# Three phases over the sequence, with Strassen's seven products in gate/up and down

## What is computed

```python
hn = rmsnorm(x, norm_mix_g)
q, k, v, r, a_low = split(hn @ w_in)                 # 512, 512, 1024, 1024, 16 columns
log_a = log_sigmoid(a_low @ w_a2 + b_a) / 16         # decays, summed up within chunks
...                                                  # scores in a chunk, a state carried from chunk to chunk
o = rmsnorm(o, gla_norm_g) * silu(r)
h = x + o @ w_out
g, u = split(rmsnorm(h, norm_ffn_g) @ w_gu)          # 2816 columns each
h = h + (silu(g) * u) @ w_down
out = rmsnorm(h, final_norm_g)
```

## Time and profile before

| | |
|---|---|
| median of 3 runs | 2424.64 us (2423.86 to 2426.31) |
| span of the profiled execution | 2424.4 us |
| TensorE busy | 2348.6 us, 97% |
| GpSimd busy | 1553.0 us, 64% |
| VectorE busy | 718.2 us, 30% |
| ScalarE busy | 539.1 us, 22% |
| mean granted TensorE clock | 0.986 of full |
| DMA | 236 MB, mean 97 GB/s |

### The profile page before, as it was taken

One profiled execution on the slowest core, in us unless ns is written; L12 is line 12 of the kernel. 1 busy time (PEld: TensorE's weight loads), 2 busy tenths in 40 slices (PEclk: granted clock), 3 DMA queues, 4 the chain that ended last, 5 costly groups with the idle time before them and its releaser, 6 DMA issues.

```text
span 2424.4 us, 33041 instructions
## 1 busy us (share of the span) xinstructions
PE 2348.6 (97%) x10948; PEld 1956.8 (81%) x10948; DVE 718.2 (30%) x1119; ACT 539.1 (22%) x871; POOL 1553.0 (64%) x1592
## 2 busy tenths in 40 slices
PE   6999999999899999999989999999998999999997
PEld 5888888888788788888778878888877888888885
DVE  5342311013534321011364431101245343110125
ACT  3331220011333222001133312200132232220114
POOL 6555677676656566677675557667766656677673
PEclk8999999999999999999999999999999999999998
DMA  4322333333422233233342223323334223332332
GB/s 142 106 65 91 96 96 102 97 95 110 135 78 78 78 108 100 96 95 95 105 140 70 86 87 99 100 96 95 95 96 139 87 72 99 98 95 96 95 97 85
DMA packets 298924, 236.26 MB, mean 97 GB/s; under 512 B 15104, under 2 KB 260864, under 8 KB 298848
## 3 DMA queue, kind: packets, MB, share of 16 engines
q1 hardware_dynamic: 290224, 209.44, 28.0%
q10 hardware_dynamic: 8624, 25.76, 2.9%
HBM read 226.76 MB, written 8.39 MB: 97 GB/s over the span
## 4 chain that ended last, share of the span: by engine, by line
PE 90%; DVE 5%; issue 2%; ACT 1%; DMA 1%; POOL 0%; DVEq 0%; ACTq 0%; POOLq 0%
PE ps L386 28%; PE ps L388 28%; PE ps L387 28%; PE ps L434 1%; PE ps L499 1%; DVE lc L909 1%; DVE xs L846 1%; PE ps L470 1%; PE ps L474 1%; DMA xs<-in_x 1%; PE ps L507 1%; DVE lc L906 1%; PE ps L443 0%; DVE newton L828 0%; PE ps L444 0%
## 5 line engine op out<-in xcount | busy, mean ns | idle before, releaser
L378 POOL TENSOR_TENSOR ring_lo<-raw,ring_hi 128x512 fp32r<-128x512 f32 x784 | 1030.6, 1315 | 65.3
L375 POOL TENSOR_SCALAR ring_hi<-raw 128x512 fp32r<-128x512 f32 x784 | 515.2, 657 | 762.8 <-PE ps L388 528.2
L386 PE MATMUL ps<-xT_hi,ring_hi 128*128 128x512 f32 (+1 forms) x1728 | 664.6, 385 | 8.3 <-DVE xT_lo L815 8.3
L387 PE MATMUL ps<-xT_lo,ring_hi 128*128 128x512 f32 (+1 forms) x1728 | 661.7, 383 | 0.0
L388 PE MATMUL ps<-xT_hi,ring_lo 128*128 128x512 f32 (+1 forms) x1728 | 661.6, 383 | 0.0
L386 PEld LDWEIGHTS ps<-xT_hi,ring_hi 128*128 128x128 f32 x1728 | 327.3, 189 | 72.1 <-issue 9.9
L388 PEld LDWEIGHTS ps<-xT_hi,ring_lo 128*128 128x128 f32 x1728 | 327.4, 189 | 62.8
L386 PE MATMUL ps<-ring_hi,act_hi 128*128 128x512 f32 x960 | 377.2, 393 | 0.8 <-POOL ring_lo L378 0.7
L387 PEld LDWEIGHTS ps<-xT_lo,ring_hi 128*128 128x128 f32 x1728 | 327.3, 189 | 62.5
L388 PE MATMUL ps<-ring_hi,act_lo 128*128 128x512 f32 x960 | 374.6, 390 | 0.0
L387 PE MATMUL ps<-ring_lo,act_hi 128*128 128x512 f32 x960 | 374.3, 390 | 0.0
(11 more groups left out here) (114 smaller groups left out, 1767.0 us busy)
## 6 DMA issues: line engine op xcount, KB each, us to landing
raw<-in_ffn_w_gu SPq DMA_DIRECT2D x352, 256.0 KB, 3.1
raw<-in_gla_w_in SPq DMA_DIRECT2D x192, 256.0 KB, 3.0
raw<-in_ffn_w_down SPq DMA_DIRECT2D x176, 256.0 KB, 3.1
raw<-in_gla_w_out SPq DMA_DIRECT2D x64, 256.0 KB, 3.0
h<-in_x ACTq DMA_DIRECT2D x16, 512.0 KB, 6.4
xs<-in_x ACTq DMA_DIRECT2D x16, 512.0 KB, 3.5
out<-xs ACTq DMA_DIRECT2D x8, 512.0 KB, 4.3
h<-in_x SPq DMA_DIRECT2D x4, 512.0 KB, 6.9
```

The lines of the kernel that those rows point to most:

```text
L375: pool.tensor_scalar(ring_hi[:, u, :], raw[:, p, u % 2, :], 1.0, 0.0, ALU.mult, ALU.add).then_inc(unit_hi[u].sem, 1)
L378: pool.tensor_tensor(ring_lo[:, u, :], raw[:, p, u % 2, :], ring_hi[:, u, :].bitcast(F32), ALU.subtract).then_inc(unit_split[u].sem, 1)
L386: pe.matmul(out, l_hi, r_hi, start=first, stop=False)
L387: pe.matmul(out, l_hi, r_lo, start=False, stop=False)
```

## The change

The program is fully unrolled and runs in three phases over the whole sequence: the mixer for all four blocks; then gate/up for all tokens; then down for all tokens, with the final norm. What passes from one to the next goes through DRAM tensors: `xop` (operands of gate/up), `hop` (hidden operands of down), `hres` (the residual). The sequence counts as NS = 2 halves of 1024 tokens.

A product of 2x2 blocks is made with seven instead of eight block products (the form of Strassen and Winograd). The blocks halve the tokens, the inner dimension and the columns. The sums of activation blocks are made once and stored with high and low parts (7 operands); the sums of weight blocks are made by GpSimd anew for each use. A "quad" is the weights for 2x2 blocks (four quarters of 128 x 512 numbers, 1 MB); its seven products take 84 matmuls. There are 44 quads in gate/up and 22 in down. Even quads of gate/up are gate, odd ones up; two make a pair. The output sums lie in PSUM banks that are used twice, so some products wait until VectorE has read a bank (`bank_free`).

GpSimd, for each quad: four sums and seven low parts.

```diff
+            def split_op(q, i):
+                pool.wait_ge(op_hi[i], q + 1)
+                pool.tensor_tensor(shaped(q, w_op[i][:, 1, :]), source(q, i), shaped(q, w_op[i][:, 0, :]).bitcast(F32),
+                                   ALU.subtract).then_inc(op_ready[i], 1)
+            for q in range(QUADS):
+                b11, b12, b21, b22 = quarters(q)
+                t2, t3 = shaped(q, w_t2[:, :]), shaped(q, w_t3[:, :])
+                pool.wait_ge(w_loaded[q % 2], 64 * (q // 2 + 1))
+                pool.tensor_tensor(t3, b22, b12, ALU.subtract).then_inc(t3_done, 1)
+                pool.wait_ge(t3_done, q + 1)
+                pool.tensor_tensor(b12, b12, b11, ALU.subtract).then_inc(t1_done, 1)
+                pool.wait_ge(t1_done, q + 1)
+                pool.tensor_tensor(t2, b22, b12, ALU.subtract).then_inc(t2_done, 1)
+                for i in range(5):
+                    split_op(q, i)
+                pool.wait_ge(op_ready[4], q + 1)
+                pool.tensor_tensor(b21, b21, t2, ALU.subtract).then_inc(t4_done, 1)
+                for i in (5, 6):
+                    split_op(q, i)
```

TensorE, gate/up:

```diff
+            def bank_free(lane, i):
+                if i == 3:
+                    pe.wait_ge(u2_done, lane + 1)
+                elif i == 4:
+                    pe.wait_ge(p1_kept, lane + 1)
+                elif i == 5:
+                    pe.wait_ge(u3_done, lane + 1)
+                elif i == 6:
+                    pe.wait_ge(c22_done, lane + 1)
+                elif lane < 2:
...
+            for q in range(U_QUADS):
+                B = q // (2 * NP)
+                for i in range(7):
+                    pe.wait_ge(op_ready[i], q + 1)
+                    if q % (2 * NP) == 0:
+                        pe.wait_ge(op_loaded[i], 64 * (B + 1))
+                    bank_free(q, i)
+                    for m in range(4):
+                        cols = slice(m * P, (m + 1) * P)
+                        ins = three(ps[:, 3 * (q % 2) + BANK[i], :], w_op[i][:, 0, cols], w_op[i][:, 1, cols],
+                                    x_op[i][:, m, 0, :], x_op[i][:, m, 1, :], m == 0 and i < 3, m == 3, i > 2)
+                    ins.then_inc(prod[i], 1)
+                    if q == 0 and i < NT:
+                        turn_result(NB - 1, i)
```

ScalarE, gate/up: the high parts of the weights, the loads of the x operands and the order of its queue (`switch` is the last quad of the first half of the tokens):

```diff
+            def op_split(q, i):
+                if i == 0 or i == 4 or i == 6:
+                    act.wait_ge(w_loaded[q % 2], 64 * (q // 2 + 1))
+                else:
+                    act.wait_ge({1: t2_done, 2: t1_done, 3: t3_done, 5: t4_done}[i], q + 1)
+                if q > 0:
+                    act.wait_ge(prod[i], lanes_end[q - 1])
...
+                split_hi(shaped(q, w_op[i][:, 0, :]), source(q, i)).then_inc(op_hi[i], 1)
+            def load_op(B, i, m):
+                act.dma_start(x_op[i][:, m, :, :].bitcast(F32), xop[B, i, :, m, :, :]).then_inc(op_loaded[i], 16)
+            def copy_p1(q):
+                act.wait_ge(prod[0], q + 1)
+                if q > 0:
+                    act.wait_ge(c21_done, q)
+                act.activation(x1[:, :], ps[:, 3 * (q % 2), :], ACT.Copy).then_inc(p1_kept, 1)
...
+            for q in range(U_QUADS):
+                B, pair = divmod(q // 2, NP)
+                pair = q // 2
+                switch = q == 2 * NP - 1
+                def next_op(i):
+                    op_split(q + 1, i)
+                    if switch:
+                        if i == 0:
+                            for slot in range(2):
+                                act.wait_ge(xop_stored[slot], 16 * (PER_BLOCK // 2) * NB)
+                        for m in range(4):
+                            load_op(1, i, m)
+                copy_p1(q)
...
+                elif q % 2 == 0:
+                    next_op(0)
+                    hidden_hi(pair - 1, 5)
+                    next_op(1)
+                    next_op(2)
+                    hidden_hi(pair - 1, 6)
+                    next_op(3)
+                    gate_silu(pair, 0)
+                    next_op(4)
+                    gate_silu(pair, 1)
+                    next_op(5)
+                    gate_silu(pair, 2)
+                    next_op(6)
+                    gate_silu(pair, 3)
+                else:
+                    next_op(0)
+                    next_op(1)
+                    if q == 1:
+                        result_granules(NB - 1, range(5, 7))
+                    next_op(2)
+                    if q == 1:
+                        result_granules(NB - 1, range(7, 10))
+                    next_op(3)
+                    if q == 1:
+                        result_granules(NB - 1, range(10, 14))
+                        for slot in range(2):
+                            act.wait_ge(xop_stored[slot], 16 * (PER_BLOCK // 2) * NB)
+                    hidden_hi(pair, 0)
+                    next_op(4)
+                    hidden_hi(pair, 1)
+                    next_op(5)
+                    hidden_hi(pair, 2)
+                    next_op(6)
+                    hidden_hi(pair, 3)
+                    hidden_hi(pair, 4)
```

VectorE, gate/up, the odd quad and the beginning of the next pair (`lane_u2` of the even one releases product 3 there):

```diff
+            def lane_u2(lane):
+                dve.wait_ge(p1_kept, lane + 1)
+                dve.wait_ge(prod[1], lane + 1)
+                dve.tensor_tensor(u2[:, :], ps[:, 3 * (lane % 2) + 1, :], x1[:, :], ALU.add).then_inc(u2_done, 1)
+            def lane_u3(lane):
+                dve.wait_ge(prod[3], lane + 1)
+                dve.tensor_tensor(u3[:, :], ps[:, 3 * (lane % 2) + 1, :], x1[:, :], ALU.add).then_inc(u3_done, 1)
+            def lane_22(lane, dst):
+                dve.wait_ge(u3_done, lane + 1)
+                dve.wait_ge(prod[2], lane + 1)
+                dve.tensor_tensor(dst[:, :], ps[:, 3 * (lane % 2) + 2, :], u3[:, :], ALU.add).then_inc(c22_done, 1)
+            def lane_21(lane, dst):
+                dve.wait_ge(prod[5], lane + 1)
+                dve.tensor_tensor(dst[:, :], ps[:, 3 * (lane % 2) + 1, :], x1[:, :], ALU.add).then_inc(c21_done, 1)
...
+            def times_gate(pair, tile, silu, ready, made):
+                dve.wait_ge(silu_done, 4 * pair + silu)
+                dve.wait_ge(ready, 2 * pair + 2)
+                dve.tensor_tensor(tile[:, :], tile[:, :], ct[:, :], ALU.mult).then_inc(made, 1)
+            def hidden_lo(pair, n):
+                number = 7 * pair + n
+                dve.wait_ge(hid_hi, number + 1)
+                split_lo(stage[number % 4][:, 1, :], (g22, g11, s1, g21, s2, g12, s4)[n][:, :],
+                         stage[number % 4][:, 0, :]).then_inc(hid_lo, 1)
+            def hidden_end(pair):
+                hidden_lo(pair, 5)
+                dve.wait_ge(hid_made, 7 * pair + 6)
+                dve.tensor_tensor(s4[:, :], g12[:, :], s2[:, :], ALU.subtract).then_inc(hid_made, 1)
+                hidden_lo(pair, 6)
...
+            for pair in range(U_QUADS // 2):
+                lane = 2 * pair
+                lane_u2(lane)
+                if pair > 0:
+                    hidden_end(pair - 1)
+                lane_u3(lane)
+                lane_22(lane, g22)
...
+                lane = 2 * pair + 1
+                lane_u2(lane)
...
+                lane_22(lane, ct)
+                times_gate(pair, g22, 1, c22_done, hid_made)
+                dve.wait_ge(silu_done, 4 * pair + 2)
+                dve.wait_ge(prod[4], lane + 1)
+                dve.tensor_tensor(g11[:, :], g11[:, :], ps[:, 3, :], ALU.mult).then_inc(c11_done, 1)
+                dve.wait_ge(c11_done, pair + 1)
+                dve.sem_inc(hid_made, 1)
...
+                hidden_lo(pair, 0)
+                hidden_lo(pair, 1)
+                lane_21(lane, ct)
+                times_gate(pair, g21, 3, c21_done, d21_done)
+                dve.wait_ge(d21_done, pair + 1)
+                dve.tensor_tensor(s1[:, :], g21[:, :], g22[:, :], ALU.add).then_inc(hid_made, 1)
+                dve.wait_ge(hid_made, 7 * pair + 3)
+                dve.tensor_tensor(g21[:, :], g11[:, :], g21[:, :], ALU.subtract).then_inc(hid_made, 1)
+                hidden_lo(pair, 2)
+                dve.tensor_tensor(s2[:, :], s1[:, :], g11[:, :], ALU.subtract).then_inc(hid_made, 1)
+                hidden_lo(pair, 3)
+                hidden_lo(pair, 4)
+                lane_12(lane, ct)
+                times_gate(pair, g12, 4, c12_done, hid_made)
+            hidden_end(U_QUADS // 2 - 1)
```

The pieces of `xop`, made in the first three heads of the next block, or for the last block in quads 0 and 1 of gate/up:

```diff
+            def result_hi(b, n):
+                kg, i = X_GRANULES[n]
+                number = PER_BLOCK * b + n
+                if i in (1, 2, 3, 6):
+                    act.wait_ge(xs_sum, 4 * (2 * b + kg) + {2: 1, 3: 2, 1: 3, 6: 4}[i])
+                else:
+                    act.wait_ge(xf_done, 2 * NT * (b + 1))
+                if number >= 2:
+                    act.wait_ge(xop_stored[number % 2], 16 * (number // 2))
+                split_hi(x_stage[b // (NB - 1)][:, number % 2, :, 0, :], x_source(kg, i)).then_inc(xop_hi, 1)
+            def result_store(b, n):
+                kg, i = X_GRANULES[n]
+                number = PER_BLOCK * b + n
```

(66 more changed lines are left out.)

## The result

The changed kernel takes **2498.5 us** (median of 4 runs, 2494.5 to 2503.0) where the kernel before, run beside it, takes 2424.3 us: a ratio of 1.031, 95% interval 1.029 to 1.032. It is slower by 74 us. The profiled execution has a span of 2496.4 us.

A forecast was written before the change was run, and what follows sets the result against it. TensorE's matmuls, with TensorE busy 97% of the span, were taken as the bound. Savings led by -179.5 us of products and added costs led by +114 summed to +77 on 2424, giving 2501 us; own range 2445 to 2560, overall 2365 to 2560.

The forecast's parts named there:

- GpSimd and VectorE in gate/up: Gate/up: GpSimd and VectorE lock each other out, making u2 late; 6.0 us in each of 19 pairs, +114 us.
- Storing the operands: Heads of the next block: ScalarE's pieces each wait for a store's landing and delay v_hi; +62 us, ends 30 and 95.
- New block borders: Between mixer blocks: late decay chain and first scaled tile, +25 us; norm_next ahead of v_lo in the last head, +27 us.
- Entry into gate/up: Start of gate/up: late weights, open norm, and last block's pieces ahead of copy_p1 on ScalarE; +38 us, ends 15 and 55.
- Change of half: After quad 21 of gate/up: reloading seven operands, 14.7 MB, takes 55 us and stops TensorE; +24 us, ends 8 and 40.
- Down: Down phase: DMA traffic fits and VectorE's gathers avoid the port, leaving 2 us for entries; +2 us, ends 0 and 45.
- Ends: Behind the last matmul: additions, squares, roots, scalings and the last store take 27 us instead of 17.4; +10 us.
- Products: Gate/up and down: 5544 matmuls instead of 6336, each 0.2267 us; -179.5 us.
- Rival 1: Gate/up: the port costs nothing because VectorE's 8.1 us chain stays inside 10.9 us; 2387 us, chance 0.17.
- Rival 2: Whole kernel: everything is covered, stores and squares too hide behind the matmuls; 2235 us, chance 0.05.
- half effect: Stores and gate/up: landing 2.9 us, 2 us stop per pair, too short to lower the clock; 2393 to 2440 us, chance 0.16.
- Rival 4: Down: DMA becomes the bound at 220 GB/s, pairs of quads taking 42 instead of 38 us; 2546 us, chance 0.12.

The follow-up runs named there:

- e1_order: Changed kernel with only VectorE's order in gate/up altered, lane_u2 of the next even quad ahead of hidden_lo 3 and 4: 2389.6 us, ratio 0.985.
- e2_no_gpsimd: Changed kernel without GpSimd's sums and low parts in gate/up from the third quad on, semaphores still raised: 2387.2 us, ratio 0.986.
- e8_both: Changed kernel with the edits of e1_order and e2_no_gpsimd together: 2385.4 us.
- e3_granules: Changed kernel with two operand pieces per head left ahead of v_hi, the others moved behind r_gate and into the recurrence's gaps: 2439.7 us, ratio 1.006.
- e4_norm: Changed kernel with three of norm_next's four multiplications moved behind v_lo in the last head of the first three blocks: 2485.7 us, ratio 1.026.
- e7_no_end: all1 without the sums, splits and stores of the last block's 14 operand pieces in the first two quads of gate/up: 2288.4 us.
- all1: Changed kernel with the order changes of e1_order, e3_granules and e4_norm together, nothing left out: 2315.6 us, ratio to before 0.955.
- e5_no_reload: all1 without the 28 loads of the second half's operands between the halves of gate/up: 2299.4 us.

## Why the prediction was right, point by point

The forecast was 2501 us, the measured median 2498.5. The sum is closer than its terms; four of them were off by more than 10 us and cancelled.

- **GpSimd and VectorE in gate/up, +114.** Right in mechanism (e1_order, e2_no_gpsimd, e8_both) and nearly in size: 19 pairs x 5.34 = 101.5 us. Inside it two parts were off in opposite ways. TensorE had finished product 2 at 1320.0, 8.3 us into the even quad, and `u2` was made at 1322.96, 11.3 us into it and not 12.6; the stop was 3.2 us, not 4.4. The clock cost 2.1 us on average, not 1.6, and from 0.1 to 3.0 us in single pairs: in the longest case it stayed at the lower level for some 6 us, against some 3 behind the 2.0 us pause of the earlier trace rows, and in two of the 19 it did not fall, so that it did not dip "in every pair". What decides between them no run here shows. The reason that the Trainium skill gives ("SBUF — State Buffer", section "SBUF: two separate sides"), that such instructions of the two engines shut each other out for a whole instruction, agrees with these runs: the same instruction takes 1.77 us beside GpSimd and 0.69 without it, and those that read PSUM take 0.68 in the same microseconds.
- **Storing the operands, +62.** 57.5 us in the trace, 58.8 given back by e3_granules. The sum for one piece was too high: a landing plus a split were counted, 4.25 us, but the split runs while the store before it is landing, and the pieces start 3.3 to 3.5 us apart. So `v_hi` starts 16.4, 13.6 and 10.4 us behind the scores in the second block's heads, against 17.5, 16 and 11.5. In the last block it is 17.7, 15.3 and 13.0 us, so that the three blocks pay 15.4, 19.0 and 23.3 us, where 21 had been set for each; why the later ones pay more is open. The whole cost was order.
- **New block borders, +25 and +27.** Too high: about 13 us a border and not 17. TensorE's waits between two blocks are 6.6 us for `v_lo`, 2.6 for the turned result and 0.5, 9.7 us in all, and 3 for the clock (99.3 us busy at 0.97). `v_lo` was late as said (6.6 against 7); e4_norm gives the border back 4.1 to 5.6 us of it. The step that failed is the first scaled tile, which the decay chain was to leave open for 5 us: TensorE does not wait for it at all, only for 2.6 us between the tiles.
- **Entry into gate/up, +38.** Too low, about 49. By the mark `s<-g,g` at 1094.93 and its place 37.3 us behind the start of an undisturbed pair (e1_order), gate/up would have had to begin at 1057.6; the output projection ended at 1004.7. Of the 52.9 us between, 3.6 are transposes counted elsewhere. e7_no_end confirms 27 us for the pieces, as predicted (28). The other item, 10 us for weights and norm, was nearer 22.
- **Change of half, +24.** 25.1 us by the marks, but the reload alone is 17.7 to 18.0 of them (e1_order, all1), and leaving it out gives back 16.2; the rest is the late `u2`, which the prediction had left out of these pairs. The loads took 49.5 us from the first issue to the last landing, not 55. The cause is the reload (e5_no_reload; 391 GB/s at a share of 1.01). What would show it was named only half rightly: the two short stops ended on the landing of an operand, the long one on `u2`, through ScalarE's queue.
- **Down, +2.** Wrong: about 19 us (447.5 us from the first to the last product, less 418.9 for 22 quads and some 9 for turned tiles). I had looked only at its DMA, which was indeed no bound (clock 1.00 and no idle from 2060 to 2200 us at 237 to 289 GB/s). Missing was the same chain of VectorE at the last pair's end, 6.0 + 4.4 us of stops and some 4 of clock (0.61 over 10.2 us of work), and three later waits for `acc`, 3.8 us. e1_order does not mend it: there the two stops are 2.7 and 6.9 us.
- **Ends, +10.** 27.0 us lie behind the last product, as worked out.
- **Products, -179.5.** Borne out: an undisturbed pair takes 38.1 us in e1_order. The -8.7 and the -49 no run measures by themselves.
- **Rivals.** Rival 1 (the port costs nothing) has the time of e1_order, 2387 against 2389.6, but not its mechanism: there too the instructions take 1.77 us, and only the order keeps TensorE free of them. Rival 2 and the half effect are excluded by the pairs and heads. The half effect also took a stop of 2 us as too short to lower the clock, against the earlier trace rows, where the clock reads 0.57 behind a pause of 2.0 us. Rival 4 falls with down, where TensorE does not stop from 2060 to 2200 us.

In numbers: -13 for the borders, -12.5 for the pairs, -4.5 for the stores, +11 for the entry, +17 for down and +1 for the change of half come to -1 us, and 2500 against a span of 2496.4; the last 3.6 us are in none of these items. That 2501 and 2498.5 lie so close is luck: terms that were off by up to 17 us cancelled.

## What to carry to other kernels

Before an engine's work is counted in microseconds, look for the one instruction that the bottleneck waits for and count only what stands ahead of it in the queue: here two instructions of 1.7 us cost 109 us in front of `lane_u2` and nothing behind it, and moving three of five stores (two of four in the third head) from in front of `v_hi` to behind `r_gate` gave back 59 us. When VectorE and GpSimd both have work with both sources in SBUF, count 1.7 us for each pair of 128x512 instructions, as measured here, and put the one that TensorE waits for first where it reads PSUM. A saving in matmuls (179.5 us here) is worth as much as the order of what surrounds it: the same instructions made 2498.5 or 2315.6 us.

## What the hardware showed that I had not expected

- The same stop of 3.1 us was followed in one pair by 6.9 us of work at a granted clock of 0.57 and in another by a clock of 1.00; over the 19 pairs the clock cost 2.1 us on average, two thirds of the stop. TensorE's busy time for the same 10040 recorded matmuls was 2247.6 us in the changed kernel and 2187.6 in all1.
- GpSimd pays too: its 1.29 us instructions took 1.62 to 1.74 us while they alternated with VectorE's.
- With more than a dozen loads of 0.5 MB under way, three more issues held ScalarE for 5.8 to 6.3 us; with 2 MB each an issue took 0.33 us, and a 0.5 MB store of another queue took 29.1 us to land, instead of 7 to 8 in the same stretch of all1; the median of all1's stores of that kind is 3.4 us.
